# A perceptron's way up: the products of two feature blocks taken in turn into two PSUM banks

## The reference

```python
def sq_relu_mlp(h, w_up, w_down):
    u = jnp.einsum('btd,df->btf', h, w_up)
    return jnp.einsum('btf,fd->btd', jnp.square(jax.nn.relu(u)), w_down)
# ...
        h = h + sq_relu_mlp(rms_norm(h, mlp_norm_g[layer]), mlp_w_up[layer], mlp_w_down[layer])
# second block:
        h = h + jnp.square(jax.nn.relu(m @ w_up[l])) @ w_down[l]
```

## Time and profile before

| | |
|---|---|
| median of 3 runs | 2169.37 us (2169.32 to 2170.28) |
| span of the profiled execution | 2165.6 us |
| TensorE busy | 2108.2 us, 97% |
| VectorE busy | 1355.1 us, 63% |
| ScalarE busy | 920.4 us, 42% |
| products of line 463, 128 x 512 | most of the 10819 instructions of TensorE |
| DMA | 83 GB/s read on average |

### The profile page before, as it was taken

One profiled execution on the slowest core, in us unless ns is written; L12 is line 12 of the kernel. 1 busy time (PEld: TensorE's weight loads), 2 busy tenths in 40 slices (PEclk: granted clock), 3 DMA queues, 4 the chain that ended last, 5 costly groups with the idle time before them and its releaser, 6 DMA issues.

```text
span 2165.6 us, 27204 instructions
## 1 busy us (share of the span) xinstructions
PE 2108.2 (97%) x10819; PEld 1670.2 (77%) x10819; DVE 1355.1 (63%) x2004; ACT 920.4 (42%) x1494; POOL 220.9 (10%) x212
## 2 busy tenths in 40 slices
PE   8999999999999999899999999999999999999998
PEld 6765668888888767688888888666878768888887
DVE  4888646867834367757687554355645435768753
ACT  3235545454443244445445442244423224544542
POOL 2210000000000011100000003020335320000000
PEclk9999999999999999999999999999999999999999
DMA  7420113233232321123333324131111313233231
GB/s 186 120 59 21 21 40 103 83 107 117 80 115 82 98 59 40 39 88 106 108 97 100 107 86 115 58 93 40 59 59 39 98 59 107 100 115 98 97 101 75
DMA packets 163511, 182.64 MB, mean 84 GB/s; under 512 B 19701, under 2 KB 123562, under 8 KB 163386
## 3 DMA queue, kind: packets, MB, share of 16 engines
q1 hardware_dynamic: 160736, 174.00, 25.6%
q0 software_dynamic: 2320, 6.80, 1.2%
q10 hardware_dynamic: 330, 0.12, 0.0%
HBM read 177.75 MB, written 2.17 MB: 83 GB/s over the span
## 4 chain that ended last, share of the span: by engine, by line
PE 86%; DVE 9%; ACT 2%; issue 2%; DMA 0%; ACTq 0%; POOLq 0%; POOL 0%; DVEq 0%
PE banks L463 72%; PE banks L2900 3%; DVE wl L398 1%; ACT wh L394 1%; PE banks L3019 1%; PE banks L1608 1%; DVE big L1292 1%; PE banks L1644 1%; DVE sm L1555 1%; PE banks L1528 1%; DVE big L1598 1%; DVE m L1290 1%; PE banks L2086 1%; PE banks L2148 1%; PE banks L2669 1%
## 5 line engine op out<-in xcount | busy, mean ns | idle before, releaser
L463 PE MATMUL banks<-uTh,wh 128*128 128x512 f32 (+1 forms) x1424 | 552.8, 388 | 9.7 <-ACT p L2021 3.6
L463 PE MATMUL banks<-uTh,wl 128*128 128x512 f32 (+1 forms) x1424 | 538.6, 378 | 0.0
L463 PE MATMUL banks<-uTl,wh 128*128 128x512 f32 (+1 forms) x1424 | 538.2, 378 | 0.0
L463 PE MATMUL banks<-wh,hTr 128*128 128x512 f32 x1552 | 488.0, 392 | 0.3 <-DVE hTr L2208 0.3
L398 DVE TENSOR_TENSOR wl<-stg,wh 128x2048 fp32r<-128x2048 f32 x133 | 306.0, 2301 | 219.0 <-ACT wh L394 218.4
L463 PEld LDWEIGHTS banks<-wh,hTr 128*128 128x128 f32 x1552 | 291.8, 188 | 64.4 <-DVE wl L398 2.5
L394 ACT ACTIVATE wh<-stg 128x2048 fp32r<-128x2048 f32 x133 | 253.0, 1902 | 194.8 <-PE banks L463 175.7
L463 PEld LDWEIGHTS banks<-uTh,wh 128*128 128x128 f32 x1424 | 268.2, 188 | 63.7 <-issue 9.5
L463 PEld LDWEIGHTS banks<-uTh,wl 128*128 128x128 f32 x1424 | 268.2, 188 | 50.9
L463 PEld LDWEIGHTS banks<-uTl,wh 128*128 128x128 f32 x1424 | 268.6, 189 | 49.3 <-issue 2.4
L463 PE MATMUL banks<-wl,hTr 128*128 128x512 f32 x776 | 302.4, 390 | 0.0
(11 more groups left out here) (383 smaller groups left out, 2793.4 us busy)
## 6 DMA issues: line engine op xcount, KB each, us to landing
stg<-mlp_w_up SPq DMA_DIRECT2D x32, 1024.0 KB, 5.3
stg<-mlp_w_down SPq DMA_DIRECT2D x26, 1024.0 KB, 5.1
stg<-w_in SPq DMA_DIRECT2D x20, 1024.0 KB, 5.2
stg<-w_up SPq DMA_DIRECT2D x16, 1024.0 KB, 5.3
stg<-w_down SPq DMA_DIRECT2D x13, 1024.0 KB, 5.1
stg<-odd_w_in SPq DMA_DIRECT2D x16, 512.0 KB, 4.8
big<-mlp_w_down SPq DMA_DIRECT2D x6, 1024.0 KB, 7.6
big<-even_cmp_w SPq DMA_DIRECT2D x4, 1024.0 KB, 5.6
```

The costliest lines, as they stand in the source:

```text
L463: t = pe.matmul(outp, x, y, start=(start and k == 0 and m == 0), stop=(stop and k == n - 1 and m == 2))
```

## The change

In `pe_up` the loop over the two blocks becomes the innermost one. For each slice k and each of the three products, block 0's product goes to bank 2g and block 1's to bank 2g + 1. Both waits for empty banks stand at the piece's start. The last two products of a piece are block 0's last and block 1's last; each raises its signal. The first piece of a perceptron and everything on the other engines stay in their order.

```diff
-                for f in range(2):
-                    j = g * 2 + f
-                    if q:
-                        pe.wait_ge(*product_taken(tag, q - 1, (4, 5, 6, 3)[j // 2], j % 2))
-                    t = fm(pe, up_bank(tag, j), w, f * 128, None)
-                    t.then_inc(*p_mm.next((tag, "up", q, j), *([("free", key)] if f else [])))
+                if q:
+                    for f in range(2):
+                        pe.wait_ge(*product_taken(tag, q - 1, (4, 5, 6, 3)[g], f))
+                for k in range(KT):
+                    uh, ul = tokens(k, 0, T)
+                    for m, (x, y) in enumerate(((w[0], uh), (w[0], ul), (w[1], uh))):
+                        for f in range(2):
+                            t = pe.matmul(up_bank(tag, g * 2 + f), x[:, k, f * 128:(f + 1) * 128], y,
+                                          start=(k == 0 and m == 0), stop=(k == KT - 1 and m == 2))
+                            if k == KT - 1 and m == 2:
+                                t.then_inc(*p_mm.next((tag, "up", q, g * 2 + f), *([("free", key)] if f else [])))
                 yield
```

## The result

| | before | changed |
|---|---|---|
| median | 2169.35 us (2168.01 to 2170.28) | 2229.94 us (2223.62 to 2233.68) |
| ratio | | 1.0278 (95%: 1.0262 to 1.0295) |
| span of the profiled execution | 2165.6 us | 2224.3 us |
| TensorE busy | 2108.2 us, 97% | 2128.6 us, 96% |
| VectorE busy | 1355.1 us | 1357.7 us |

The forecast was 2226.7 with a range of 2207 to 2241. The profiled execution took 2226.5 us.

A forecast was written before the change was run, and what follows sets the result against it. TensorE, busy 97%, was taken to bound the kernel. Hand-over waits 32.9, round 3 7.9 and clock 16.5 sum to 57.3 us, put on the 2169.4 median: 2226.7 us, range 2207 to 2241.

The forecast's parts named there:

- Cadence: 2160 alternating products: spacing unchanged, zero; bounds a gain of at most 28.8 us and no loss.
- Rivals 2 and 4: Products cheaper: whole fixed part back, 2198 us (chance 0.06); or overlap beyond it, 2147 us at 190 ns (0.03).
- Waits moved to the piece's start: Both banks waited for at a piece's start: zero, covered by more than 8 us.
- Between pieces: Way up: ScalarE and VectorE need 7.2 us behind a piece, TensorE wants it after 10.9; zero, slack 3.7 us.
- P1, 3.5 us per round: Way up to way down, rounds 0 to 2: TensorE waits 3.5 us for combined weights, plus 0.15; 32.9 us.
- Round 3: Start of its way down: first product waits 2.62 us for the last piece's a part, three times; 7.9 us.
- Clock: Granted clock falls after most of TensorE's new idles in the perceptrons: 16.5 us, bounds zero and 41.
- Rival 1: Same TensorE waits as forecast, but the clock is kept: 2210 us; chance 0.16.
- Rival 3: Waits grow: two slow stretches per idle, or a second idle at P2 or P5; 2249 us; chance 0.10.

## Why the prediction was right, step by step

- **Cadence: zero.** Right. 226.7 ns before, 226.7 after. The single pairs across a bank change in the trace of before told it. Nothing of the 13.3 ns that don't depend on the columns was gained. The page "TensorE: Matmul & The Clock Gate" of the Trainium skill, section "Back-to-back issue gap", with about 216 ns for an isolated gap, stays below what this kernel shows in either order. Rivals 2 and 4 are out.
- **Waits moved to the piece's start: zero.** Right as far as the trace shows: none of them is among TensorE's waits.
- **Between pieces: zero, slack 3.7 us.** Right for TensorE, but incomplete. The kernel with all but the last piece in turn showed that piece 2's late end alone costs 1.0 us per perceptron, since VectorE then starts s3 1.4 us later. In the changed kernel this is hidden: there VectorE idles for 3.37 us before s3.
- **P1, 3.5 us per round, with 0.15 at P2.** Measured 3.56 at P1 and about 0.1 at P2, with 0.1 for the restart (the first product after the wait stands 0.34 us ahead of the second), which I had not counted. The cause, t1 and t2 queued behind the last piece's a, was shown for 3.1 us of it by moving only these two. The other 0.45 would be there without them, since the late relu holds ScalarE's high part of P1 as well.
- **Round 3, 2.62 us.** Measured 2.72: part a was there 2.62 us late, as forecast, and TensorE's first product followed 0.10 us behind it.
- **Clock, 16.5 us.** Measured some 17 by the changed kernel's trace (18.1 with restarts and P2), and 17 to 18 by the filled idles. The mechanism and the size were right. It was the term with the widest bounds (0 to 41), and it rested on two rows, one with a fall and one without. A fall was not sure at any one place: 10 of 12. That the sum came so near is in part luck.
- Sum 57.3 against 58.7 in the span and 60.6 between the medians. The four runs lie up to 10 us apart, at granted clocks of 0.983 to 0.988; six stretches of half clock more or less would do that.
- Rival 1 (same waits, clock kept) is what the kernel with filled idles makes real: 2213, where I had 2210. Rival 3 came true once, at 1029.2, and no more.

## What to carry to other kernels

Where the last of several results is made in halves, an order that finishes both halves together takes half of the making time away from whatever is built on the first. Look on each consumer for what is queued behind the first use of that half; here it was weight sums that didn't need it at all, and moving them ahead gave back 44 of the 60 us. On an engine that is busy all the time an idle costs its length and, at 2.6 to 3.4 us, another 1.4 to 1.5 us on average by the clock (17 to 18 us over 12 idles).

## What I had not expected of the hardware

- Two idles of the same length, 3.4 us, in the same surroundings: behind the first the clock stayed, behind the second it fell for 3.4 us, and at one of the twelve for 6.8. In the kernel with only the last piece in turn, whose twelve idles are the same, the first one was followed by a fall, and there were 13 such stretches at 11 idles:

```profile
399.60:403.40 3.80, 0.40 (x3) 0.01 (x1) 3.80 (x3) 2.20 (x3) 0.00 (x0) 1.00 0.78 274
403.90:407.30 3.40, 3.40 (x9) 2.64 (x9) 2.02 (x4) 3.14 (x4) 0.00 (x0) 0.50 0.00 0
```

So a single execution doesn't tell what an idle costs.
- The first product after one of these waits costs more than 0.227 us to the next one, also at full clock: 0.34 at P1 (402.87 to 403.21 above) and 0.31 at the start of round 3's way down (656.16 to 656.47).
- Products of 128 x 512 keep their distance of 226.7 ns whether the bank and the stationary block change at every product or not, within 1 ns.
